# Moving the scan's preparation into the convolution and p's projection into the stage that chooses tokens, in a one-layer encoder kernel

## The reference, cut to what matters

```python
proj = u @ w_in                                   # q, k, v, z, xbc, dt
xbc = silu(depthwise_conv(xbc, 3 taps) + conv_b)  # 1280 channels -> x (1024), B, C (128 each)
dt = softplus(dt_raw + dt_bias); A = -exp(a_log)  # 16 heads, forward and backward
a = dt * A; acum = cumsum(a, within chunks of 128 tokens)
states = B^T (x * dt * exp(acum_last - acum))     # one state per chunk, then carried from chunk to chunk
gates = sigmoid(u @ w_gate + b_gate)              # used to merge attention and scan
...
aff = softmax(u2 @ w_router); top_k per expert    # expert choice, 16 experts
...
ple_gate = sigmoid(h @ w_ple_gate + b_ple_gate)   # 1024 x 1024
h = h + ple_gate * (p @ w_ple_proj)               # p has 256 columns per token
return rmsnorm(h, g_final)
```

## Time and profile before

| | us |
|---|---|
| median of three runs (3291.61 to 3296.46) | 3293.35 |
| the profiled execution | 3291.5 |
| span of its trace | 3289.5 |
| PE busy | 2752.9 (84%) |
| DVE busy | 1652.2 (50%) |
| ACT busy | 1262.2 (38%) |
| POOL busy | 300.9 (9%) |

### The profile page before, as it was taken

How to read it: one execution, slowest core, us unless ns; L and a number is a source line. 1 busy time by engine, 2 the same in 40 slices (tenths; PEclk the granted TensorE clock), 3 DMA queues, 4 the chain that set the end, 5 groups by cost and what they waited for, 6 DMA issues and landing times. The chain is left out here.

```text
span 3289.5 us, 42094 instructions
## 1 busy us (share of the span) xinstructions
PE 2752.9 (84%) x15560; PEld 2359.9 (72%) x15560; DVE 1652.2 (50%) x2158; ACT 1262.2 (38%) x1791; POOL 300.9 (9%) x346
## 2 busy tenths in 40 slices
PE   3999999894677279687996991799999999998696
PEld 2789888683556157576784880799999999997575
DVE  5100000523888687540664228577777777776324
ACT  4111111322566445331442110355555555554222
POOL 1000000100001200020110000001111010101122
PEclk6999999897889699898998995699999999999798
DMA  8412120644310334573875540478878787885312
GB/s 272 115 64 89 71 85 39 201 145 124 92 34 11 89 95 127 162 259 106 293 252 186 191 153 2 149 237 250 252 234 259 245 251 239 248 246 156 110 40 101
DMA packets 446372, 515.88 MB, mean 157 GB/s; under 512 B 18280, under 2 KB 386808, under 8 KB 445400
## 3 DMA queue, kind: packets, MB, share of 16 engines
q1 hardware_dynamic: 414304, 390.10, 38.5%
q0 software_dynamic: 31968, 124.44, 11.9%
HBM read 392.65 MB, written 121.83 MB: 156 GB/s over the span
## 5 line engine op out<-in xcount | busy, mean ns | idle before, releaser
L2033 DVE TENSOR_TENSOR ex_w_lo<-ex_w_raw,ex_w_hi 128x2048 fp32r<-128x2048 f32 x195 | 443.9, 2291 | 142.9 <-ACT ex_w_hi L1990 142.9
L2122 PE MATMUL ex_ps_u<-ex_x,ex_w_hi 128*128 128x384 f32 x2048 | 411.1, 341 | 5.1 <-DVE ex_w_lo L2033 5.1
L1990 ACT ACTIVATE ex_w_hi<-ex_w_raw 128x2048 fp32r<-128x2048 f32 x195 | 370.4, 1909 | 0.8
L2122 PEld LDWEIGHTS ex_ps_u<-ex_x,ex_w_hi 128*128 128x128 f32 x2048 | 348.7, 189 | 6.1 <-issue 5.5
L2122 PEld LDWEIGHTS ex_ps_u<-ex_x,ex_w_lo 128*128 128x128 f32 x2048 | 265.5, 191 | 0.6
L2141 PE MATMUL ex_ps_d<-ex_w_hi,ex_h 128*128 128x512 f32 x768 | 265.8, 400 | 0.0
L2122 PE MATMUL ex_ps_u<-ex_x,ex_w_lo 128*128 128x192 f32 x2048 | 265.5, 272 | 0.0
L354 DVE TENSOR_TENSOR w_lo<-w_raw,w_hi 128x2048 fp32r<-128x2048 f32 x15 | 34.3, 2290 | 404.1 <-ACT w_hi L322 404.1
L328 ACT ACTIVATE stage<-ps 128x512 f32<-128x512 f32 (+1 forms) x102 | 55.9, 548 | 414.9 <-PE ps L376 359.5
L2141 PE MATMUL ex_ps_d<-ex_w_lo,ex_h 128*128 128x512 f32 x512 | 202.9, 396 | 0.0
L2141 PEld LDWEIGHTS ex_ps_d<-ex_w_hi,ex_h 128*128 128x128 f32 x768 | 144.6, 188 | 35.0
(11 more groups left out here) (380 smaller groups left out, 5188.0 us busy)
## 6 DMA issues: line engine op xcount, KB each, us to landing
ex_w_raw<-in_w_exp_gate SPq DMA_DIRECT2D x64, 1024.0 KB, 5.2
ex_w_raw<-in_w_exp_up SPq DMA_DIRECT2D x64, 1024.0 KB, 6.1
ex_w_raw<-in_w_exp_down SPq DMA_DIRECT2D x64, 1024.0 KB, 6.5
w_raw<-in_w_in SPq DMA_DIRECT2D x15, 1024.0 KB, 5.7
mg_w_raw<-in_w_ssm_up SPq DMA_DIRECT2D x24, 512.0 KB, 5.7
mg_g_raw<-g_d SPq DMA_DIRECT2D x24, 512.0 KB, 7.1
xbcT_d<-stage POOLq DMA_DIRECT2D x5, 1536.0 KB, 5.6
cv_raw<-xbcT_d POOLq DMA_DIRECT2D x10, 768.0 KB, 5.7
```

The costliest lines, as they stand in the source:

```text
L1990: act.activation(w_hi[:, j % CUT], w_raw[:, j % RAW], ACT.Copy).then_inc(w_hi_done, 1)
L2033: dve.tensor_tensor(w_lo[:, j % CUT], w_raw[:, j % RAW], w_hi[:, j % CUT].bitcast(F32), ALU.subtract).then_inc(w_split, 1)
L2122: last = pe.matmul(ps_u[:, j % 2, m, 0:wide * C], w[:, s, k, cols], x[:, k, 0:wide].rearrange("p a c -> p (a c)"), start=i == 0, stop=i == ...
```

## The change

There are four edits. In `convolve` the SiLU, the turns and the copy of channel tile m move from step m to step m+5 (LATE), and the scan's preparation is put around and between the first gate units: SP loads dt, its bias, `a_log` and the triangles between the first two weight tiles; DVE runs the preparation's steps before conv(0), with split_lo(0) after the third and split_lo(1) after the last; ACT waits for those constants and takes the exponentials; PE forms the sums behind unit 2 and turns them behind units 3 and 4; SP stores the four decay parts. `wgt` and the chunk totals `etot` stay in SBUF until the scan. In `scan_ssm` the preparation is gone, the first chunk of x is loaded ahead of the constants, the zeroing goes from POOL to ACT, and ACT lays its constants between the state copies of chunks 0 to 6. In `choose_tokens` p (transposed on the host, 1.5 MB) and `w_ple_proj` (1 MB) are loaded, split into hi on ACT and lo on POOL, and multiplied in 24 halves of six matmuls on PE, placed in its queue between the turns of the logits and those of the places; ACT copies each half out and SP stores it to DRAM. In `embed_and_norm` a tile's load is h and its 512 KB of that product instead of h and 128 KB of p, a turn has eight transposes instead of ten, a half 24 matmuls instead of 30, the weights' splits eight row blocks instead of ten, and `mix` reads the product from SBUF instead of PSUM.

```diff
+    LATE = 5
+    STEPS = max(XT + LATE, NG)
...
+            dve.memset(ones[:], 1.0).then_inc(ones_set, 1)
+            dve.wait_ge(consts_in, 64)
+            p = Chain(dve, prep)
+            every = lambda t: t[:].unsqueeze(1).to_broadcast([P, NC, 2 * H])
+            p.step(dve.tensor_tensor(dtr[:], dtr[:], every(dtb), ALU.add))
+            p.step(dve.tensor_scalar(mag[:], dtr[:], -1.0, None, ALU.mult))
+            p.step(dve.tensor_tensor(mag[:], dtr[:], mag[:], ALU.max))
+            split_lo(0)
+            dve.wait_ge(prep_exp, 2)
+            p.step(dve.tensor_scalar(num[:], ex[:], 2.0, None, ALU.add))
...
+            p.step(dve.scalar_tensor_tensor(out=a_[:], in0=dts[:], scalar=-1.0, in1=every(amp), op0=ALU.mult, op1=ALU.mult))
+            p.step(dve.tensor_scalar(num[:], dts[:], 1.0e-37, None, ALU.max))
+            split_lo(1)
             conv(0)
-            split_lo(0)
-            for n in range(1, XT):
+            dve.wait_ge(prep_exp, 4)
+            dve.tensor_tensor(wgt[:], rest[:], dts[:], ALU.mult)
+            dve.wait_ge(prep_exp, 6)
+            dve.tensor_tensor(be[:], be[:], acs[:], ALU.subtract).then_inc(be_made, 1)
+            conv(1)
+            dve.wait_ge(aT_hi, 1)
+            dve.tensor_tensor(aT[:, 1], turns(0), aT[:, 0].bitcast(F32), ALU.subtract).then_inc(aT_lo, 1)
+            split_lo(2)
+            conv(2)
+            dve.wait_ge(bT_hi, 1)
+            dve.tensor_tensor(bTs[:, 1], turns(1), bTs[:, 0].bitcast(F32), ALU.subtract).then_inc(bT_lo, 1)
+            for n in range(3, XT):
                 conv(n)
-                if n % NB == NB - 1:
-                    split_lo(n // NB + 1)
-            for t in range(XT // NB + 1, NTL):
+                if n % NB == 1:
+                    split_lo((n + LATE) // NB)
...
-            act.preload_act_table(ACT.Silu)
+            act.preload_act_table(ACT.Exp)
...
+            act.wait_ge(consts_in, 64)
+            act.activation(amp[:], alog[:], ACT.Exp).then_inc(prep_exp, 1)
             split_hi(0)
+            act.wait_ge(prep, 3)
+            act.activation(ex[:], mag[:], ACT.Exp, scale=-1.0).then_inc(prep_exp, 1)
             for n in range(STEPS):
                 s = n % 2
...
+                m = n - LATE
...
+                if n == 2:
+                    act.wait_ge(sums_done, 3)
+                    act.activation(acs[:], sums(ACUM), ACT.Copy).then_inc(prep_exp, 1)
+                    act.activation(rest[:], sums(REST), ACT.Exp).then_inc(prep_exp, 1)
+                    act.activation(etot[:], sums(TOT), ACT.Exp).then_inc(prep_exp, 1)
+                    act.wait_ge(prep, PREP)
+                    act.activation(be[:], num[:], ACT.Ln).then_inc(prep_exp, 1)
+                    act.preload_act_table(ACT.Silu)
...
+                if n == 2:
+                    pe.wait_ge(ones_set, 1)
+                    pe.wait_ge(prep, PREP - 1)
+                    for b, w in ((ACUM, (0, 1)), (REST, (2, 3))):
+                        for d in range(2):
+                            last = pe.matmul(sums(b)[:, :, d * H:(d + 1) * H], tri[:, w[d]], a_[:, :, d * H:(d + 1) * H], start=True, stop=True)
+                        last.then_inc(sums_done, 1)
+                    pe.matmul(sums(TOT), ones[:], a_[:], start=True, stop=True).then_inc(sums_done, 1)
...
-            for t in range(2):
-                load_w(t)
+            load_w(0)
+            for out, src in ((dtr[:], dt_d.rearrange("(c p) h -> p c h", p=P)), (dtb[:], dt_bias.to_broadcast([P, 2 * H])), (alog[:], a_log.to_broadcast([P, 2 * H])), (tri[:], tri_d)):
+                sp.dma_start(out, src).then_inc(consts_in, 16)
+            load_w(1)
...
-            for out, src in ((tri[:], tri_d), (dtb[:], dt_bias.to_broadcast([P, 2 * H])), (alog[:], a_log.to_broadcast([P, 2 * H])), (dtr[:], dt_d.rearrange("(c p) h -> p c h", p=P)), (dsk[:], d_skip.to_broadcast([P, H])), (idn[:], ident)):
+            sp.dma_start(x_in[:, 0], xb_d[0][:, 0:D + P]).then_inc(x_landed[0], 16)
+            for out, src in ((idn[:], ident), (dsk[:], d_skip.to_broadcast([P, H])), (tri[:], tri_d)):
                 sp.dma_start(out, src).then_inc(consts_in, 16)
-            for c in range(XR):
+            for c in range(1, XR):
...
-            dve.wait_ge(consts_in, 96)
...
             weigh(0)
...
-        @block.gpsimd
-        def _(pool):
-            pool.wait_ge(ones_set, 1)
-            pool.tensor_scalar(bst[:].rearrange("p c d j -> p (c d j)"), ones[:, 0:1].to_broadcast([P, NC * 2 * P]), 0.0, None, ALU.mult).then_inc(zeroed, 1)
-            pool.tensor_scalar(mov[:].rearrange("p s i -> p (s i)"), ones[:, 0:1].to_broadcast([P, 2 * H * P]), 0.0, None, ALU.mult).then_inc(zeroed, 1)
...
+            act.wait_ge(ones_set, 1)
+            act.activation(bst[:].rearrange("p c d j -> p (c d j)"), ones[:, 0:1].to_broadcast([P, NC * 2 * P]), ACT.Copy, scale=0.0).then_inc(zeroed, 1)
+            act.activation(mov[:].rearrange("p s i -> p (s i)"), ones[:, 0:1].to_broadcast([P, 2 * H * P]), ACT.Copy, scale=0.0).then_inc(zeroed, 1)
+
+            def lay_rates():
+                act.wait_ge(zeroed, 2)
+                for d in range(2):
+                    at = d * SN + 2 * H
+                    act.activation(bst[at:at + 2, :, d], ones[at:at + 2].unsqueeze(1).to_broadcast([2, NC, P]), ACT.Copy)
+
+            def lay_heads(s):
+                act.wait_ge(picked, 1)
                 for d in range(2):
                     rows = slice(d * SN, d * SN + 2 * H)
                     last = act.activation(mov[rows, s].rearrange("p (h i) -> p h i", i=P), pick[rows].unsqueeze(2).to_broadcast([2 * H, H, P]), ACT.Copy)
...
+                last.then_inc(laid, 1)
+
+            def lay_sides():
+                act.wait_ge(consts_in, 48)
+                act.activation(idr[:], idn[:], ACT.Copy).then_inc(idr_made, 1)
+                act.wait_ge(sel_in, 64)
+                act.activation(sel[:], sel_raw[:], ACT.Copy).then_inc(skip_made, 1)
+
+            def scale_skip(h0, h1):
+                for h in range(h0, h1):
+                    last = act.activation(dskI[:, h], idn[:], ACT.Copy, scale=dsk[:, h:h + 1])
+                last.then_inc(skip_made, 1)
...
+                if c == 0:
+                    lay_rates()
+                    lay_heads(0)
+                if c == 1:
+                    lay_heads(1)
+                if c == 2:
+                    lay_sides()
+                if 3 <= c < 7:
+                    scale_skip(4 * (c - 3), 4 * (c - 2))
...
+            sp.dma_start(p_raw[:], pT).then_inc(p_in, 16)
+            sp.dma_start(w_raw[:], w_ple_proj.rearrange("(k p) d -> p k d", p=P)).then_inc(wp_in, 16)
+            for n, (t, c) in enumerate(HALVES):
+                sp.wait_ge(e_copied, n + 1)
+                sp.dma_start(ple_d[t][:, c * BLK:(c + 1) * BLK], e_out[:, n % 4]).then_inc(e_out_done[n % 4], 16)
+            for done in e_out_done:
+                sp.wait_ge(done, 16 * len(HALVES) // 4)
...
+        @block.gpsimd
+        def _(pool):
+            pool.wait_ge(p_hi_done, 1)
+            pool.tensor_tensor(p_lo[:], p_raw[:], p_hi[:].bitcast(F32), ALU.subtract).then_inc(p_split, 1)
+            pool.wait_ge(wp_hi_done, 1)
+            pool.tensor_tensor(w_lo[:], w_raw[:], w_hi[:].bitcast(F32), ALU.subtract).then_inc(wp_split, 1)
...
+            act.wait_ge(p_in, 16)
+            act.activation(p_hi[:], p_raw[:], ACT.Copy).then_inc(p_hi_done, 1)
+            act.wait_ge(wp_in, 16)
+            act.activation(w_hi[:], w_raw[:], ACT.Copy).then_inc(wp_hi_done, 1)
+            for n in range(len(HALVES)):
+                act.wait_ge(e_full, n + 1)
+                if n >= 4:
+                    act.wait_ge(e_out_done[n % 4], 16 * (n // 4))
+                act.activation(e_out[:, n % 4], ps_e[:, n % 2], ACT.Copy).then_inc(e_copied, 1)
...
+            for n, (t, c) in enumerate(HALVES):
+                if n == 0:
+                    pe.wait_ge(wp_hi_done, 1)
+                    pe.wait_ge(p_hi_done, 1)
+                if n >= 2:
+                    pe.wait_ge(e_copied, n - 1)
+                terms = [(v, w, k) for v, w in ((p_hi, w_hi), (p_lo, w_hi), (p_hi, w_lo)) for k in range(KP)]
+                for i, (v, w, k) in enumerate(terms):
...
+                    last = pe.matmul(ps_e[:, n % 2], v[:, k, t * P:(t + 1) * P], w[:, k, c * BLK:(c + 1) * BLK], start=i == 0, stop=i == len(terms) - 1)
+                last.then_inc(e_full, 1)
...
-                sp.dma_start(rows[:, KT:KA, cols], w_p[:, :, cols]).then_inc(w_in[c], 16)
...
-                    pool.dma_start(hp[:, s, D:D + PLE], p[tile]).then_inc(landed[s], 16)
+                    pool.dma_start(hp[:, s, D:2 * D], ple_d[tile]).then_inc(landed[s], 16)
...
-                dve.tensor_tensor(z[:, c], sig[:, c], ps_p[:, c], ALU.mult).then_inc(mixed, 1)
+                dve.tensor_tensor(z[:, c], sig[:, c], hp[:, s, D + c * BLK:D + (c + 1) * BLK], ALU.mult).then_inc(mixed, 1)
...
```

(43 more changed lines are left out.)

252 lines of the change are left out of this document (110 added, 142 removed).

## The result

The changed kernel takes 3265.28 us (median of four runs, 3262.6 to 3267.17) against 3294.57 for the kernel before in the same comparison: ratio 0.9912, 95% interval 0.9899 to 0.9924. That is 29.3 us less, where 30.5 less were forecast. A second set of five runs of the same kernel gave 3267.76 and a ratio of 0.9921 (0.9908 to 0.9935). The profiled execution has a span of 3263.4 instead of 3289.5, 26.1 less; the execution profiled before was the fastest of its runs, so the traces show less of the gain than the medians.

What follows compares the result with a forecast made beforehand. PE was taken to bound the convolution and nearly the embedding, and preparation, then DVE, to pace the scan. Scan -39.2, convolution +2.6, choosing 0, embedding +6.1 sum to -30.5: 3263 us from median 3293.35, range 3241 to 3279.

Steps and rivals of the forecast that it cites:

- the likeliest case: Whole kernel: the summed terms hold, -30.5 us to 3263 us; chance 0.55.
- The scan, -39.2 forecast: Scan: preparation gone from its start, ACT's zeroing and lays the new limit; -38.2 and -1.0 us.
- the -1.0 taken: Scan's end: the Exp table load goes, no Ln ahead of it; -1.0 us out of 0 to -1.28.
- Rival E: Scan: ACT zeroes at POOL's 2.6 ns per column, carry(2) waits 11.9 us longer; 3275 us; chance 0.08.
- The convolution, +2.6 forecast: Convolution: products 2.2, transposes 0.8, later start 2.4, minus the 2.85 us w_lo wait; range +1 to +7.
- landing after 4.35 like the weights: Convolution's start: last constant, issued at about 605.8, lands 4.35 us later; w_hi at 610.4, +2.4 us.
- Choosing, 0 forecast: Choosing stage: 24 halves, 33 us, fit PE's idle time before the places' turn; POOL's splits leave DVE unharmed; 0.
- Rival C: Choosing stage: POOL's splits hold DVE's rounds, +13.3 us, giving 3276 us; chance 0.08.
- The embedding, +6.1 forecast: Embedding, ten tiles: -6.7 us less work on the path, +17.7 clock falls, -4.9 at the head.
- 1.77 was taken: Embedding loop: price in us per clock fall, eight matmuls taking 3.75 us at low clock against 1.98 at high.
- Rival B: Embedding: the clock holds, PE's gap too short or the load landing as early as before; 3245 us; chance 0.25.
- Rival D: Embedding: loads of 1 MB per tile land late, ahead of the turn; slower, 3300 us; chance 0.04.

Runs made afterwards that it cites:

- the spread lays: Changed kernel with ACT's scan lays spread so no chunk has more than one half of a lay of heads behind its copies: 3268.32 us, ratio 0.9925.
- The edit of two orders: Changed kernel with the first gate weights rounded and split ahead of the wait for the four constants, on ACT and DVE: 3262.15 us, ratio 0.9907.
- the filled gap: Changed kernel with twelve unread 128x512 matmuls more per embedding tile, between half 0 and the turn: 3253.87 us, ratio 0.9883.
- the run with h alone: Changed kernel whose embedding turn waits only for h, the product's load having its own semaphore, for which the mix waits: 3248.01 us, ratio 0.9859.

## Why the prediction was right

The time (3263 forecast, 3265.28 measured), its sign and the likeliest case hold. Point by point:

- **The scan, -39.2 forecast, -42.3 measured.** The chain of ACT's lays and DVE's carries came out as worked out: 57.3 us to the last copy instead of 57.9, with carry(2) 25.7 us after the stage's first issue (26.1 forecast). That the carries wait for ACT is shown by the brackets and by the spread lays, which removed DVE's two waits. The rest is behind that point: -3.4 instead of the -1.0 taken. The table load is gone, and PE's first outputs are faster (a group of four in 0.44 us after, 0.70 before): in the kernel before TensorE's granted clock fell there (0.66 from 1185 to 1190), in the changed one it held (1.00 from 1154 to 1159). The prediction had no term for that. Rival E is out: ACT's rate was 0.89 ns per column.
- **The convolution, +2.6 forecast, +7.2 measured.** The step that failed is "landing after 4.35 like the weights". The last of the constants is there at 614.17, not at about 610.15 (605.8 + 4.35): the issue of the second took 2.15 us instead of 0.43, and the last landed 7 us after its issue. The edit of two orders gave 7.1 us back. The other terms held: the five products took 1.46 + 0.81 (2.2 forecast), the turns 0.98 (0.8), and the wait for w_lo went; a part of that 2.85 us was lost again because the second eight matmuls still ran at the low clock (3.16 instead of 2.15).
- **Choosing, 0 forecast, +1.2 measured.** Rival C is out: the max did not change. The 1.2 us come from a cost that the prediction had put at nothing, the loads behind the constants; with p's load held back the stage takes 112.40.
- **The embedding, +6.1 forecast, +6.4 measured.** The gap of 3.9 us was met, and so was the fall of the clock, and the filled gap shows that the fall is the price: 1.8 us per tile, where 1.77 was taken. The price is right, its make-up only in part: it was taken from eight matmuls at the low level, and in the trace some 0.9 of it lies in the transposes (1.97 instead of 1.09) and the rest in the matmuls behind them. From the second tile's turn to the last the stage takes 10.1 us more (11.0 forecast), and outside that 3.8 less (4.9). Rival B needed a shorter gap; the run with h alone shows that at 2.5 to 2.8 us it would have been about half right. Rival D is out: the loads landed 4.4 us after their issue.

The errors of the convolution (+4.6) and of the scan (-3.1) partly cancel, by luck; the sum is better than its terms.

## What to carry to other kernels

Ask of work that is taken off an engine whether the engine was the bound there or waited in a loop of its own: the same removal lost 6 us where a load two buffers deep set the pace, and was worth 35 where four buffers had made the engine the bound. When work is moved ahead of a stage's first instruction, put it behind that instruction on every queue that it shares with it; the runs show this for ACT's and DVE's. And ahead of cutting an engine's work in a loop with a gap, look at what the longer gap does to the clock.
